# A hybrid encoder of two layers on one core: attention scores by alternating row halves, masks in PSUM, exponentials by pairs of heads

## What is computed

```python
scores = einsum('bnqkgd,bnskd->bnkgqs', qb, kb) * HEAD_DIM ** -0.5
valid = (abs(qpos - kpos) <= WINDOW) & (kpos >= 0) & (kpos < s)
scores = where(valid, scores, NEG_INF)
m = maximum(max(scores, axis=-1, keepdims=True), sink_b)
p = exp(scores - m)
denom = sum(p, axis=-1, keepdims=True) + exp(sink_b - m)
probs = p / denom
out = einsum('bnkgqs,bnskd->bnqkgd', probs, vb)
```

## Time and profile before

| | |
|---|---|
| median of 3 runs | 1280.42 us (1280.05 to 1280.5) |
| profiled execution | 1281.08 us, its span 1279.6 us |
| TensorE busy | 1248.1 us, 98% |
| TensorE weight loads busy | 971.8 us, 76% |
| VectorE busy | 580.5 us, 45% |
| ScalarE busy | 434.2 us, 34% |
| DMA | 419.50 MB, mean 328 GB/s |

### The profile page before, as it was taken

The page is one execution under the profiler, slowest core; times in us unless marked ns, Lnnn a source line. Parts: engine busy times, 40 slices in busy tenths (PEclk is TensorE's granted clock), DMA queues, the critical chain, the costliest instruction groups (busy, mean ns, idle before and its releaser), DMA issues.

```text
span 1279.6 us, 31530 instructions
## 1 busy us (share of the span) xinstructions
PE 1248.1 (98%) x14347; PEld 971.8 (76%) x14347; DVE 580.5 (45%) x931; ACT 434.2 (34%) x674; POOL 10.8 (1%) x35
## 2 busy tenths in 40 slices
PE   7999999999998999999999999999999999999997
PEld 6788888888787776777777777766677778768894
DVE  5696545546596655664766647521100012210003
ACT  7565444446563444543544535300000000000002
POOL 3000000000000000000000000000000000000000
PEclk9999999999998999999999999999999999999999
DMA  9335844274103999999999999999999999999993
GB/s 341 139 132 197 300 165 173 85 263 156 43 1 118 422 420 421 421 424 423 419 423 419 423 423 419 421 422 421 421 415 417 401 393 399 414 419 420 424 420 139
DMA packets 109018, 419.50 MB, mean 328 GB/s; under 512 B 4632, under 2 KB 8768, under 8 KB 100688
## 3 DMA queue, kind: packets, MB, share of 16 engines
q1 hardware_dynamic: 107776, 416.30, 80.5%
q0 software_dynamic: 544, 1.12, 0.3%
q10 hardware_dynamic: 560, 0.01, 0.0%
HBM read 416.37 MB, written 1.05 MB: 326 GB/s over the span
## 4 chain that ended last, share of the span: by engine, by line
PE 80%; DMA 11%; DVE 5%; ACT 3%; issue 1%; SPq 0%; DVEq 0%
PE bank L2225 25%; PE bank L2289 12%; PE bank L1845 12%; PE bank L1846 12%; PE bank L1847 12%; DMA ring<-in_moe_w_down 6%; DMA ring_after<-in_moe_w_down 2%; DMA ring<-in_moe_w_up 2%; PE bank L2154 2%; PE bank L2160 2%; ACT raw_d L870 1%; DVE lo L1195 1%; DVE mx L1285 1%; DVE raw_d L1282 1%; ACT w_hi L804 1%; PE bank L1924 1%
## 5 line engine op out<-in xcount | busy, mean ns | idle before, releaser
L1637 DVE TENSOR_TENSOR w_lo<-ring,w_hi 128x896 fp32r<-128x896 f32 (+2 forms) x192 | 202.2, 1088 | 80.8 <-ACT w_hi L804 74.8
L2225 PE MATMUL bank<-ring,late_acts 128*32 128x224 f32 x4736 | 234.0, 353 | 0.0
L2225 PEld LDWEIGHTS bank<-ring,late_acts 128*32 128x32 f32 x4736 | 189.1, 110 | 40.7 <-issue 5.0
L804 ACT ACTIVATE w_hi<-ring 128x896 fp32r<-128x896 f32 (+2 forms) x192 | 176.0, 948 | 118.2 <-PE bank L1847 73.3
L1065 ACT ACTIVATE silu_buf<-bank 128x224 f32<-128x224 f32 (+2 forms) x76 | 29.1, 394 | 433.9 <-PE bank L2225 433.9
L1845 PE MATMUL bank<-hi,act_hi 128*128 128x512 f32 (+1 forms) x400 | 155.5, 389 | 2.8 <-DVE act_lo L1220 1.8
L1846 PE MATMUL bank<-lo,act_hi 128*128 128x512 f32 (+1 forms) x400 | 153.5, 384 | 0.0
L1847 PE MATMUL bank<-hi,act_lo 128*128 128x512 f32 (+1 forms) x400 | 153.4, 384 | 0.0
L1195 DVE TENSOR_TENSOR lo<-raw_gu,hi 128x1024 fp32r<-128x1024 f32 x96 | 113.7, 1222 | 47.6 <-ACT hi L804 47.5
L1660 DVE TENSOR_TENSOR silu_buf<-silu_buf,bank 128x224 f32<-128x224 f32 (+2 forms) x76 | 32.0, 435 | 207.3 <-PE bank L2225 186.0
L804 ACT ACTIVATE hi<-raw_gu 128x1024 fp32r<-128x1024 f32 x96 | 97.7, 1059 | 38.9 <-PE bank L1847 35.3
(11 more groups left out here) (249 smaller groups left out, 1349.1 us busy)
## 6 DMA issues: line engine op xcount, KB each, us to landing
ring<-in_moe_w_up SPq DMA_DIRECT2D x59, 1792.0 KB, 20.3
ring<-in_moe_w_gate SPq DMA_DIRECT2D x58, 1792.0 KB, 20.2
ring<-in_moe_w_down SPq DMA_DIRECT2D x53, 1792.0 KB, 20.4
ring_after<-in_moe_w_down SPq DMA_DIRECT2D x11, 1792.0 KB, 19.6
raw_gu<-in_w_in SPq DMA_DIRECT2D x7, 2048.0 KB, 12.3
raw_gu<-in_dense_w_gate SPq DMA_DIRECT2D x5, 2048.0 KB, 7.9
raw_gu<-in_dense_w_up SPq DMA_DIRECT2D x5, 2048.0 KB, 12.5
raw_d<-in_dense_w_down SPq DMA_DIRECT2D x5, 2048.0 KB, 14.5
```

The lines of the kernel that those rows point to most:

```text
L804: return nc.scalar.activation(out, in_, ACT.Copy, **kw)
L1637: v.tensor_tensor(w_lo[:, n % WP, 0:b - a], flat(u)[:, a:b], w_hi[:, n % WP, 0:b - a], ALU.subtract).then_inc(w_lo_done, 1)
L2225: ins = mm(bank[b][32 * c:32 * c + 32, 0:n], acts[STEPS[s][0]][:, k, g.col:g.col + 32], w[:, c], start=k == 0, stop=k == KT - 1)
```

## The change

It reorders the score matmuls of `scores`: for c from 0 to 3, the head c of key head 0 and then the head c of key head 1, so that instructions on partitions 0 to 63 and 64 to 127 alternate; the banks become complete in the order 0, 2, 1, 3 (`SCORE_BANKS`). `masked_scores` adds the mask in PSUM, in place, on the 128 columns per head of the partly visible key block alone, without the scale; it reduces each bank from PSUM and computes at once the negative bias of its two heads from the scaled maximum and the negative sink `nsink`, and releases ScalarE for that bank. `nsink` is a new constant of 16 columns, computed once by VectorE in `rope` of layer 0, and its buffer is allocated last. `exps` waits for each bank, takes the scores from PSUM with the scale in the activation, and waits for `sinkd` on a semaphore of its own. `turn_probs` waits for pairs of heads. On VectorE `probT_copy` of block 0 moves ahead of the z products and the denominators.

```diff
+        nsink = sb("nsink", [P, 2, NH])
...
+        SCORE_BANKS = (0, 2, 1, 3)
...
             def exps(layer, t):
-                act.wait_ge(masked_done, 2 * layer + t + 1)
-                for h in range(NH):
-                    nc.scalar.activation(prob[:, h * 256:(h + 1) * 256], prob[:, h * 256:(h + 1) * 256], ACT.Exp,
-                                         bias=nmx[:, t, h:h + 1], accum_out=psums[:, t, h:h + 1]).then_inc(exp_done, 1)
+                for n, b in enumerate(SCORE_BANKS):
+                    act.wait_ge(masked_done, 4 * (2 * layer + t) + n + 1)
+                    for i in range(2):
+                        h = 2 * b + i
+                        nc.scalar.activation(prob[:, h * 256:(h + 1) * 256], bank[b][:, i * SEQ:(i + 1) * SEQ], ACT.Exp,
+                                             bias=nmx[:, t, h:h + 1], scale=HD ** -0.5,
+                                             accum_out=psums[:, t, h:h + 1]).then_inc(exp_done, 1)
+                act.wait_ge(sinkd_done, 2 * layer + t + 1)
                 nc.scalar.activation(esink[:, t, :], sinkd[:, t, :], ACT.Exp).then_inc(exp_done, 1)
...
+                    link(v.tensor_scalar(nsink[:, :, :], sink_sb[:, :, :], -1.0, None, ALU.mult))
...
             def masked_scores(layer, t):
 
                 i = 2 * layer + t
-                for b in range(4):
-                    dve.wait_ge(scores_done, 4 * i + b + 1)
-                    two_heads = prob[:, b * 512:(b + 1) * 512].rearrange("p (h n) -> p h n", h=2)
-                    link(v.scalar_tensor_tensor(
-                        out=two_heads, in0=bank[b][:, :].rearrange("p (h n) -> p h n", h=2), scalar=HD ** -0.5,
-                        in1=mask[:, t, :].unsqueeze(1).to_broadcast([P, 2, SEQ]), op0=ALU.mult, op1=ALU.add))
-                    ins = v.tensor_reduce(mx[:, 2 * b:2 * b + 2], two_heads, AX, ALU.max)
-                link(ins)
-                link(v.tensor_tensor(mx[:, :], mx[:, :], sink_sb[:, layer, :], ALU.max))
-                v.tensor_scalar(nmx[:, t, :], mx[:, :], -1.0, None, ALU.mult)
-                v.tensor_tensor(sinkd[:, t, :], sink_sb[:, layer, :], mx[:, :], ALU.subtract).then_inc(masked_done, 1)
+                edge = slice(P, SEQ) if t == 0 else slice(0, P)
+                for n, b in enumerate(SCORE_BANKS):
+                    dve.wait_ge(scores_done, 4 * i + n + 1)
+                    two = slice(2 * b, 2 * b + 2)
+                    two_heads = bank[b][:, :].rearrange("p (h n) -> p h n", h=2)
+                    link(v.tensor_tensor(two_heads[:, :, edge], two_heads[:, :, edge],
+                                         mask[:, t, edge].unsqueeze(1).to_broadcast([P, 2, P]), ALU.add))
+                    link(v.tensor_reduce(mx[:, two], two_heads, AX, ALU.max))
+                    v.scalar_tensor_tensor(out=nmx[:, t, two], in0=mx[:, two], scalar=-HD ** -0.5,
+                                           in1=nsink[:, layer, two], op0=ALU.mult, op1=ALU.min).then_inc(masked_done, 1)
+                dve.wait_ge(masked_done, 4 * (i + 1))
+                v.tensor_tensor(sinkd[:, t, :], sink_sb[:, layer, :], nmx[:, t, :], ALU.add).then_inc(sinkd_done, 1)
...
                 pieces(16, 18)
+                probT_copy(layer, 0)
...
                 denominators(layer, 0)
-                probT_copy(layer, 0)
                 pieces(18, 22)
...
             def scores(layer, t):
 
-                for b in range(4):
-                    for i in range(2):
-                        h = 2 * b + i
-                        rows = slice(HD * (h // 4), HD * (h // 4) + HD)
-                        ins = mm(bank[b][:, i * SEQ:(i + 1) * SEQ], qT[rows, h % 4, t * P:(t + 1) * P],
+                for c in range(4):
+                    for g in range(NKV):
+                        b, i = 2 * g + c // 2, c % 2
+                        rows = slice(HD * g, HD * g + HD)
+                        ins = mm(bank[b][:, i * SEQ:(i + 1) * SEQ], qT[rows, c, t * P:(t + 1) * P],
                                  kT[rows, :], start=True, stop=True)
-                    ins.then_inc(scores_done, 1)
+                        if i == 1:
+                            ins.then_inc(scores_done, 1)
 
             def turn_probs(layer, t):
 
-                for h in range(NH):
-                    pe.wait_ge(exp_done, (NH + 1) * (2 * layer + t) + h + 1)
-                    for kt in range(NT):
-                        c = (h % 2) * 256 + kt * P
-                        ins = tr(bank[h // 2][:, c:c + P], prob[:, h * 256 + kt * P:h * 256 + kt * P + P], ident[:, :])
+                for n, b in enumerate(SCORE_BANKS):
+                    pe.wait_ge(exp_done, (NH + 1) * (2 * layer + t) + 2 * n + 2)
+                    for h in (2 * b, 2 * b + 1):
+                        for kt in range(NT):
+                            c = (h % 2) * 256 + kt * P
+                            ins = tr(bank[b][:, c:c + P], prob[:, h * 256 + kt * P:h * 256 + kt * P + P], ident[:, :])
                 ins.then_inc(probT_done, 1)
```

## The result

The changed kernel takes 1271.77 us (median of 5 runs, 1271.12 to 1273.15) against 1280.05 us of the kernel before in the same comparison: 8.3 us less between the medians. The ratio is 0.9939, 95% interval 0.9928 to 0.9949, which is some 7.8 us less. The profiled execution took 1271.47 us, its span is 1270.0 us.

The account below looks back on a forecast made before the run. TensorE bounds the front part, and the expert stage is a DMA stream starting after routing. Per layer 0.85 + 1.15 + 0.40 + 0.85 + 0.35 = 3.60 us, twice 7.2, from 1280.42 to 1273.2 us; range 1271.8 to 1276.3.

Parts of the forecast that it names:

- The expert stage follows the routing: Expert stage, some 875 us: starts when routing ends and runs at its own pace, so earlier routing moves the end equally.
- Scores, 0.85 us per call: Score matmuls on TensorE: alternating row halves runs all 16 at the pace of the old middle, saving 0.85 us per call.
- The first rival: Score matmuls: they start strictly in program order, so alternation gains only about 0.2 us per call; 1275.8 us, chance 0.12.
- The first turn, 1.15 us: Turning block 0's probabilities on TensorE: no waits remain, 1.92 us instead of 3.07, 1.15 us gained.
- VectorE's 1.27 us per bank: Masks and maxima on VectorE: mask add, reduction from PSUM, small operation and semaphore waits take 1.27 us per bank.
- The wait ahead of the scores of block 1, 0.40 us: TensorE before block 1's scores: the wait for VectorE's copy of block 0's turned probabilities goes, 0.40 us gained.
- The section on the order on VectorE: VectorE's queue: block 0's probability copy moves ahead of z products and denominators, is ready in time, and gains 0.40 us.
- The values of block 1, 0.35 us: Value matmuls of block 1: copies of its probabilities start at once when the transposes end, saving 0.35 us.
- the margin: Before the copy of block 1's probabilities: VectorE is free only about 0.35 us before the transposes end.
- a sign of being wrong: Before the values of block 1: TensorE waiting for VectorE's copy by more than 0.5 us would show the forecast wrong.
- The slower rival: Masks and maxima: PSUM halves VectorE's rate, 2.08 us per bank, 2.5 us lost per layer, 1285.4 us; chance 0.04.
- The routing rival: Behind the routing, 404 to 424 us: the shift lengthens the low-clock stretch, in full giving 1276.6 us; chance 0.05.

Follow-up runs that it names:

- halves in turn: The changed kernel with the score matmuls in the old order, rows 0 to 63 first and banks 0, 1, 2, 3: 1275.94 us.
- alternation by bank: The changed kernel with score matmuls alternating by whole banks, four instructions on the lower rows, then four on the upper: 1271.45 us.
- The runs with delays: The changed kernel with an extra VectorE reduction per bank: 512 columns, both blocks 1292.19 us, block 1 only 1285.39; 256 columns, both 1286.23, block 1 only 1279.17.
- the second reduction in both blocks: The changed kernel with each bank's reduction of all 512 columns done twice on VectorE, in both blocks: 1292.19 us.

## Why the prediction was right, and where it was not

The forecast was 1273.2 us, 7.2 us less; measured are 1271.77 us and 7.8 us less by the ratio. That is 0.03 us under the lower end of the range, 1271.8, which is far less than the runs spread. Part of the distance is no merit or fault of the sum: the median of before came out 0.37 us under the 1280.42 that the forecast started from, and the medians differ by 8.3 us where the two pairs of profiles differ by 7.65 and 7.81 us in the middle stretch. The rest lies within the spread of the runs. Step by step:

*The expert stage follows the routing.* Right: in the 14 profiles it is between 873.2 and 874.3 us long, whenever it starts, from 395.45 to 415.93 us. The first expert load came at 396.42 us instead of the 398.3 foreseen; 1.46 us of that is the start.

*Scores, 0.85 us per call.* Measured 0.96 in block 0 (2.89 to 1.93) and 0.93 in block 1 (2.86 to 1.93). The mechanism was right and the size too small. The slow start, 0.97 us against 0.85 for four, is a first distance between two matmuls of one half of 0.32 us instead of 0.216; before, the two halves pay it one after the other, now at the same time. I had named this as the upper bound, 0.95 us. Four calls make 0.38 us, most of the missing 0.6. The first rival falls: halves in turn and alternation by bank both deny a strict order of matmuls. The rule of the Trainium skill, page "TensorE: Matmul & The Clock Gate", section "Part 3: Packing small matmuls", that matmuls start in program order, does not hold for these matmuls on different row halves: by the estimate from this case's 0.216 and 0.108 us a call by banks would take 3.0 us under it, and it took 2.03.

*The first turn, 1.15 us.* Measured 1.16 (3.07 to 1.91), and VectorE's 1.27 us per bank was measured as 1.26 to 1.28, with PSUM as cheap as SBUF (0.69 us for the reduction from either).

*The wait ahead of the scores of block 1, 0.40 us.* It is gone, but I credited the wrong edit. The section on the order on VectorE let it hang on the moved copy; with the copy at its old place it is gone as well, because the exponentials' early end brings VectorE's whole queue forward. The gain is of 0.47 us, since 64.88 must be compared with the start that a call has without a wait, 64.41 (0.32 us behind the matmul at 64.09, as 60.79 is behind 60.47 in the changed kernel):

```profile
64.09 0.39 PE L1847 MATMUL bank<-hi,act_lo 128*128 128x512 f32 x1
```

*The values of block 1, 0.35 us, and the margin.* Right: the start of the values is bound by the copies, as said, and comes 3.39 us behind the start of the turn instead of 3.73. TensorE waits there, 0.51 us. That just passes the 0.5 us that I had named as a sign of being wrong, but VectorE was not late: its copies started at 74.75 us, as the transposes ended, 0.23 us after it was free. The sign was set too tight, since the wait follows from the copies alone. VectorE's margin was this 0.23 us, not 0.35.

*The sum as a sum.* It is right for the whole change and for the masks and exponentials alone (1.15 + 0.40 + 0.35, twice 1.9 us foreseen, 4.0 measured), but not for the alternation alone. I gave each scores call its 0.85 us as time on the path, because TensorE "goes straight on to work whose inputs are ready"; in the kernel before that is false two stages later, where the inputs are not ready, and the alternation alone is worth 0.0 us. The text held the condition, that the exponentials be ready when TensorE turns them, but not what the part is worth without it.

*The slower rival.* Its place was right and its price far too low. I let it turn the change into a loss from 3.6 us of delay per layer, 1.76 us per bank. The runs with delays show 1279.17 us already at 1.5 us per layer (before on the same chip 1280.66), and losses below 3.6: 1285.39 us at 2.6 and 1286.23 at 3.35 (before 1281.07, one run each), because a longer wait of TensorE ahead of the values brought 1.2 GHz with it. At 1.99 us per bank, which the second reduction in both blocks gives, that rival's sum comes to 1284.0 us by my estimate, and 1292.19 was measured. I had looked for the clock at the routing and not at the wait that this very rival makes.

*The routing rival.* No effect found. In the first profile of the changed kernel the clock is lower for longer around the routing, 0.76 on the mean of 20 us instead of 0.83, but the stage behind it is 873.6 us long, against 874.1; and in the second profile of the same kernel the mean is 0.83 as before, so that the longer stretch is not the change's. The stretch in the two profiles of the changed kernel:

```profile
395.00:415.00 20.00, 17.72 (x101) 16.01 (x102) 15.12 (x46) 9.62 (x17) 0.00 (x0) 0.76 0.89 346
```

```profile
396.00:416.00 20.00, 17.45 (x106) 15.62 (x106) 15.96 (x47) 10.59 (x18) 0.00 (x0) 0.83 0.88 339
```

## What to carry to other kernels

Follow the chain before pricing a part: work cut from an engine that next waits for another was worth nothing here (0.0 us) until the other's work was cut too, and 3.8 us with it. Such cuts must be tried together. When matmuls use half of the array's rows, alternate the halves so that one's weight load lies beside the other's matmul; here two matmuls then took the 0.216 us of one. When a change can lengthen a wait of TensorE, price the clock with it and look at the granted clock in the profile: here a fall cost 3.2 to 4.9 us on top of delays of 1.5 to 5.5 us.

## What the hardware showed that was not expected

- A wait of TensorE of 3.07 to 3.15 us ahead of the values brought 1.2 GHz in all six cases (two layers of three kernels), a wait of 2.0 us in one of two. The fall came between 1.2 us before the end of the wait and 1.7 us after it, and lasted some 7 or 10 us. After the waits of 0.51 us of the changed kernel the clock stayed. A fall cost 3.2 to 4.9 us each.
- Two streams of 64-row matmuls in f32, each with its own weight load, run at 0.108 us per instruction (two starts every 0.216 us), half of the 0.216 of one stream. Matmuls of one half start ahead of up to three waiting ones of the other, so the halves may also change only after four instructions (2.03 us per call instead of 1.93).
- Exponentials that read PSUM take 0.47 us for 256 columns, those that read SBUF 0.49 us, in place.
- The moment at which the clock first rises differs between executions of the same program: at 15.7 and 10.0 us in the two profiles of the kernel before, at 8.8 and 15.1 us in those of the changed kernel.
